# RWKV-7 time mixing on TensorE: key and value products on the off-diagonal quarters, state-free products beside the inverse

## What is computed

```python
def step(s, inp):
    r_t, w_t, k_t, v_t, kk_t, a_t = inp
    sa = jnp.einsum('bhvk,bhk->bhv', s, -kk_t)
    s = (s * w_t[:, :, None, :] + sa[..., None] * (kk_t * a_t)[:, :, None, :]
         + v_t[..., None] * k_t[:, :, None, :])
    return s, jnp.einsum('bhvk,bhk->bhv', s, r_t)
```

## Time and profile before

| | us |
|---|---|
| median of three runs | 5607.72 (5603.7 to 5607.86) |
| the profiled execution | 5603.66 |
| its span, first to last instruction | 5601.9 |

### The profile page before, as it was taken

The page is one execution under the profiler, slowest core; times in us unless marked ns, Lnnn a source line. Parts: engine busy times, 40 slices in busy tenths (PEclk is TensorE's granted clock), DMA queues, the critical chain, the costliest instruction groups (busy, mean ns, idle before and its releaser), DMA issues. The chain is left out here.

```text
span 5601.9 us, 109510 instructions
## 1 busy us (share of the span) xinstructions
PE 5508.0 (98%) x47116; PEld 5411.2 (97%) x47116; DVE 3766.9 (67%) x5137; ACT 2192.3 (39%) x2817; POOL 1360.0 (24%) x902
## 2 busy tenths in 40 slices
PE   8999999999999999989999999999999999999999
PEld 7898999999999999989999999999999999999998
DVE  5676653232357633258887777777778988989898
ACT  4343332222223322122233333334345565555555
POOL 1000000000002200016688888888500000000000
PEclk9999999999999999999999999999999999999999
DMA  3111122232337743323345555555554344353432
GB/s 116 41 54 54 40 94 94 91 115 84 112 107 263 260 155 138 107 82 68 93 100 138 125 116 125 121 123 119 168 191 165 133 150 155 135 177 122 165 133 81
DMA packets 291684, 687.83 MB, mean 123 GB/s; under 512 B 109280, under 2 KB 125024, under 8 KB 268832
## 3 DMA queue, kind: packets, MB, share of 16 engines
q1 hardware_dynamic: 187952, 616.90, 32.5%
q0 software_dynamic: 96128, 45.17, 6.2%
q10 hardware_dynamic: 7152, 19.15, 0.9%
HBM read 564.94 MB, written 116.02 MB: 122 GB/s over the span
## 5 line engine op out<-in xcount | busy, mean ns | idle before, releaser
L2418 POOL DMA_INDIRECT gate_rows<-ah_shares,ah_cells x576 | 1071.4, 1860 | 186.8 <-issue 178.6
L2902 PE MATMUL ps<-va_h_high,va_v_high 128*128 128x288 f32 x3584 | 1056.6, 295 | 6.4 <-DVE va_h_low L140 4.9
L2904 PE MATMUL ps<-va_h_high,va_v_low 128*128 128x288 f32 x3584 | 1058.0, 295 | 0.0
L2903 PE MATMUL ps<-va_h_low,va_v_high 128*128 128x288 f32 x3584 | 1056.9, 295 | 0.0
L2902 PEld LDWEIGHTS ps<-va_h_high,va_v_high 128*128 128x128 f32 x3584 | 673.4, 188 | 7.0 <-DVE va_v_low L140 5.1
L2904 PEld LDWEIGHTS ps<-va_h_high,va_v_low 128*128 128x128 f32 x3584 | 673.5, 188 | 0.0
L2903 PEld LDWEIGHTS ps<-va_h_low,va_v_high 128*128 128x128 f32 x3584 | 673.4, 188 | 0.0
L140 DVE TENSOR_TENSOR ah_ul<-ah_u,ah_uh 128x1024 fp32r<-128x1024 f32 (+1 forms) x344 | 449.6, 1307 | 316.1 <-ACT ah_uh L2359 291.8
L2359 ACT CAST ah_uh<-ah_u 128x1024 fp32r<-128x1024 f32 x324 | 339.8, 1049 | 510.3 <-PE ps L2285 501.0
L2284 PE MATMUL ps<-hn_low,ah_uh 128*128 128x288 f32 x1728 | 511.5, 296 | 0.0
L2285 PE MATMUL ps<-hn_high,ah_ul 128*128 128x288 f32 x1728 | 510.8, 296 | 0.0
(11 more groups left out here) (538 smaller groups left out, 13957.2 us busy)
## 6 DMA issues: line engine op xcount, KB each, us to landing
ah_u<-peer_u SPq DMA_DIRECT2D x216, 512.0 KB, 4.9
va_v<-peer_v SPq DMA_DIRECT2D x96, 1024.0 KB, 7.7
ret_w<-w_ret SPq DMA_DIRECT2D x46, 1024.0 KB, 4.9
gate_rows<-mo_zeros POOLq DMA_DIRECT2D x128, 288.0 KB, 3.9
h_kept<-ah_h SPq DMA_DIRECT2D x128, 288.0 KB
va_g<-gate_rows SPq DMA_DIRECT2D x60, 576.0 KB, 5.7
ah_hidden<-h_kept SPq DMA_DIRECT2D x60, 576.0 KB, 4.9
ah_v<-peer_v SPq DMA_DIRECT2D x30, 1024.0 KB, 5.0
```

What stands on the lines that cost most here:

```text
L2418: pool.indirect_dma_start(cell, bass.IndirectOffsetOnAxis(ap=source[0:m, n, k:k + 1], axis=0), shares[0:m, n, k:k + 1], None, compute_op=A ...
L2902: pe.matmul(z, ah[:, r, f], th[:, q, r, :], start=begin, stop=False, skip_group_check=True)
L2903: pe.matmul(z, ah[:, r, f], tl[:, q, r, :], start=False, stop=False, skip_group_check=True)
L2904: done = pe.matmul(z, al[r][:, f], th[:, q, r, :], start=False, stop=r == R - 1, skip_group_check=True)
```

## The change

Four things, all in `rwkv_stage`.

1. A second helper, `cross`, puts head 0's rows on columns 64 to 127 and head 1's on 0 to 63, the two other quarters. The products of keys and values go there: `kf·pq` in the x phase, the transposes of `kf` and `vs`, `xm·v`, `k·v`. Their results stand with the heads swapped, and the later ones, whose operands are swapped, swap them back.
2. The transposes leave the x phase. The plan of the inverse grows from 14 to 20 products: `tb`, `tk`, `tv` (transposes), `rv`, `yv` (`xm·v` for R and for Y) and `kv` (`k·v`). A product of the five crossed ones stands in one *turn* with the one ahead of it, and a turn's two products alternate chunk by chunk, each in its own bank. ACT evacuates `tb`, `tk`, `tv`; DVE evacuates `rv`, `kv`, `yv` (`kv` times the decay at the chunk's end).
3. The chain loses `k·v` and both `xm·v`. DVE adds their stored results instead: in R and S the `TENSOR_SCALAR` becomes a `SCALAR_TENSOR_TENSOR`, and Y is a DVE addition where ACT copied. R of chunk 0 needs no product. Of the samples, `s8` and one of the two products of `sV` go, and DVE has one more addition in chunk 3.
4. The three pieces after U7 move to x2, x4 and x6, one each. DVE's identity minus `edge` (L967 before) waits for the last `tk`, since it overwrites `kf`.

```diff
     return [
+        ("tb", "pb", "I", "b", None, None),
+        ("tk", "pk", "I", "k", None, None),
         ("f2", "F", "f", "A", "G", None),
+        ("tv", "pv", "I", "v", None, None),
         ("F2", "f", "F", "B", None, None),
         ("f4", "B", "A", "E", None, None),
+        ("rv", "x2", "v", "rv", None, None),
         ("F4", "A", "B", "H", "J", None),
         ("D1", "G", "IF", "L", None, None),
+        ("kv", "k", "v", "kv", None, None),
...
         ("h", "L", "G", "B", None, None),
+        ("yv", "x3", "v", "yv", None, None),
         ("Z", "J", "B", "Z", None, None),
...
-        by_vector = ("F2", "D2", "DT")
-        products = [(n, g) for n in range(len(plan)) for g in range(len(groups))]
+        by_vector = ("F2", "D2", "DT", "rv", "kv", "yv")
+        turns = [[n, n + 1] if n + 1 < len(plan) and plan[n + 1][0] in crossed else [n]
+                 for n in range(len(plan)) if plan[n][0] not in crossed]
+        products = [(n, g) for turn in turns for g in range(len(groups)) for n in turn]
...
-        after = {"a": 4, "g": 2, "ss": 8, "bon": 8, "x": 2, "U1": 4, "U3": 4, "U5": 3, "U7": 3, "Y7": 8, "yT": 2}
+        after = {"a": 4, "g": 2, "ss": 8, "bon": 8, "x2": 1, "x4": 1, "x6": 1, "x": 2, "U1": 4, "U3": 4, "U5": 3, "Y7": 8, "yT": 2}
...
-                for c in range(NCH - 1):
-                    act.wait_ge(pe_s.sem, pe_s.of(i, f"Y{c}"))
-                    act.copy(yy[:, c, :], X[2][:, 0:HEAD]).then_inc(a_s.step(f"Y{c}"), 1)
...
+            def cross(out, lhs, rhs, start=True, stop=True):
+                for r, q in zip(ROWS2, ROWS2[::-1]):
+                    last = pe.matmul(out[q], lhs[r], rhs[r], start=start, stop=stop)
+                return last
...
                     both(x[:, 0:C], pq[:, c, 0, :], part(bb, c))
-                    both(x[:, C:3 * C], part(bb, c), right)
-                    both(x[:, 3 * C:5 * C], part(kf, c), right)
...
-                    both(y[:, 0:C], part(bb, c), eye[:, :])
-                    both(y[:, C:2 * C], part(kf, c), eye[:, :])
-                    both(y[:, 2 * C:3 * C], part(vs, c), eye[:, :]).then_inc(pe_s.step(f"x{c}"), 1)
+                    cross(y[:, C:3 * C], part(kf, c), right)
+                    both(x[:, C:3 * C], part(bb, c), right).then_inc(pe_s.step(f"x{c}"), 1)
+                    if f"x{c}" in after:
+                        fill(i, f"x{c}")
...
-                    both(X[3][:, 0:HEAD], b, uu, start=False).then_inc(pe_s.step(f"S{c}"), 1)
-                    both(X[2][:, 0:HEAD], xm[:, c, 1, :], uu, start=False).then_inc(pe_s.step(f"Y{c}"), 1)
-                    if c < NCH - 2:
-                        both(X[0][:, 0:HEAD], xm[:, c + 1, 2, :], tok[:, c + 1, 2, :], stop=False)
+                    both(X[3][:, 0:HEAD], b, uu, start=(c == 0)).then_inc(pe_s.step(f"S{c}"), 1)
+                    both(X[2][:, 0:HEAD], xm[:, c, 1, :], uu, start=(c == 0)).then_inc(pe_s.step(f"Y{c}"), 1)
...
-                    dve.tensor_scalar(st[:, (c + 1) % 2, :], X[3][:, 0:HEAD], winc[:, end:end + 1], None, ALU.mult)\
-                        .then_inc(v_s.step(f"S{c}"), 1)
-                    dve.drain()
-                dve.wait_ge(a_s.sem, a_s.of(i, f"Y{NCH - 2}"))
+                    dve.scalar_tensor_tensor(out=st[:, (c + 1) % 2, :], in0=X[3][:, 0:HEAD], scalar=winc[:, end:end + 1],
+                                             in1=kv[:, c, :], op0=ALU.mult, op1=ALU.add).then_inc(v_s.step(f"S{c}"), 1)
+                    dve.wait_ge(pe_s.sem, pe_s.of(i, f"Y{c}"))
+                    dve.tensor_tensor(yy[:, c, :], X[2][:, 0:HEAD], yv[:, c, :], ALU.add).then_inc(v_s.step(f"Y{c}"), 1)
+                    dve.drain()
```

More of the change, by code:

```diff
@@ L302, in rwkv_stage @@
         mats = {x: by_chunk(y) for x, y in zip("ABEGHJL", (rs, ks, kk, at, sg, cs, cse))}
+        mats |= {x: tok[:, :, n, :] for n, x in enumerate("bkv")}
+        mats |= {"rv": by_chunk(dif), "kv": by_chunk(vs), "yv": by_chunk(rs)}
+        crossed = ("tk", "tv", "rv", "kv", "yv")
         def part(x, c):
@@ L762, in _ @@
+                    both(x[:, C:3 * C], part(bb, c), right).then_inc(pe_s.step(f"x{c}"), 1)
+                    if f"x{c}" in after:
+                        fill(i, f"x{c}")
                 fill(i, "x")
-                for j, (n, g) in enumerate(products):
-                    name, l, r, _, _, _ = plan[n]
+                for turn, g in [(turn, g) for turn in turns for g in range(len(groups))]:
                     by_act, by_dve = [], []
-                    if j >= 4:
-                        before = label(*products[j - 4])
-                        if before in to_act:
-                            by_act += [before]
-                        else:
-                            by_dve += [before]
-                    elif j >= 2:
-                        by_act += [f"tv{NCH - 1}"]
-                    for m in (l, r):
-                        by = [k for k in range(n) if m in plan[k][3:6]]
-                        if by:
-                            lab = label(by[-1], g)
-                            if m == plan[by[-1]][3] and plan[by[-1]][0] not in by_vector:
-                                by_act += [lab]
-                            else:
-                                by_dve += [lab]
-                    if n == 0:
-                        by_dve += ["il"]
@@ new lines, in _ @@
+                    for n in turn:
+                        name, l, r, _, _, _ = plan[n]
+                        j = turn_no[n, g]
+                        if j >= 4:
+                            before = label(*products[j - 4])
+                            if before in to_act:
+                                by_act += [before]
+                            else:
+                                by_dve += [before]
+                        else:
+                            by_dve += [f"mx{NCH - 1}"]
+                        for m in (l, r):
+                            by = [k for k in range(n) if m in plan[k][3:6]]
+                            if by:
+                                lab = label(by[-1], g)
+                                if m == plan[by[-1]][3] and plan[by[-1]][0] not in by_vector:
+                                    by_act += [lab]
+                                else:
+                                    by_dve += [lab]
+                            elif m == "IF":
+                                by_dve += ["il"]
```

94 lines of the change are left out of this document (51 added, 43 removed).

## The result

| | before | changed |
|---|---|---|
| median of five runs each, us | 5603.7 (5595.36 to 5607.86) | 5637.99 (5629.72 to 5642.51) |
| the profiled execution, its span | 5603.66, 5601.9 | 5639.64, 5637.8 |
| ratio, changed to before | | 1.006 (95%: 1.0045 to 1.0075) |

The kernel became slower by 34 us, 0.6%. That lies in the range given (5602 to 5650) and on the side that was given 60%, but it is nearly four times the 9 us of the case held likeliest, and outside that case's own range (5608 to 5626).

The account below looks back on a forecast made before the run. PE, busy 98% of the span, was taken as the bound. Per pair, x phase -1.5, inverse +5.4 and chain -2.8 us gave +1.1, +9 in all: 5617 us against the median, with 8 in 10 from 5602 to 5650.

Parts of the forecast that it names:

- B: Rival: only wide products overlap, so the inverse pays for crossed products; +2.9 us a pair, 5631 us; chance 20%.
- C: Rival: crossed products wait for their partners in x phase and inverse; +4.7 us a pair, 5645 us; chance 21%.
- case A: Likeliest case: four quarters run at once, crossed products cost nothing; +1.1 us a pair, 5617 us (5608 to 5626); 45%.
- Four quarters at once: PE array: a crossed product beside its partner costs nothing (likelier) or its full time, 0.22 us wide, 0.12 narrow.
- x phase: Before the inverse: cheaper chunks, three single pieces added; 8.7 us against 10.2, minus 1.5 a pair.
- Chain: Last of the three stages costed: round trips over DVE shorten little, minus 2.8 us a pair in all.
- U7 to S7: End of the chain: without the pieces after U7 this step falls from 2.83 us to 0.66, minus 2.17.
- R0: Start of the chain: rn comes from stored rv, so U0 stands 0.05 us behind the sample product, minus 0.82.
- Case D: Rival, faster: removed products shorten the chain (2.4 us a pair) or half the bank waits go (2.2); 5598 or 5580; 12%.
- The waits for banks: Inverse: PE waits for evacuations because turns fill two of four banks per group; 4.05 us walked, 4.4 taken.
- The inverse: Twenty products in fifteen turns: one more turn 1.05 us, crossed products 0, bank waits 4.4; plus 5.4 a pair.
- The clock: Closing remark: a granted clock below 1.00 in these stages would make the forecast wrong; no size or chance given.

## Why the prediction was right in sign and short in size

The measured 5638 us lies inside the stated range by luck. The range went up to 5650 to make room for B and C, in which crossed products cost time, and they don't; case A, whose mechanism held, ended at 5626. The same goes for the side: 41 of the 60% for slower came from B and C, and A alone leaned to no difference. What made the kernel slower by so much were two terms that the sum didn't have.

- **Four quarters at once: right.** Price of a crossed product beside its partner: nothing. Partners start 0.01 us apart on the same rows, the wide ones of the x phase (231.79 and 231.80) and the narrow ones of the inverse (243.86 and 243.87, [f4,rv]), and a group of both narrow products takes 0.36 us. B and C fall, although the median came out between their two times (5631 and 5645): their longer groups are found only in the run with all products on the diagonal.
- **x phase: right,** -1.3 for -1.5.
- **Chain: right,** -2.9 for -2.8, with its parts: U7 to S7, R0, and nothing for the products between R and U. Case D falls with that.
- **The waits for banks: right.** Second pair: 1.3 + 1.09 + 0.75 + 1.5 is 4.6 us, against 4.05 walked and 4.4 taken; and the run with another order on DVE took two of them away.
- **The inverse: a term was missing.** Plus 6.9 where 5.4 was said. Nearly all of the difference is the supply of instructions, 1.4 us a pair, 11 us in all. The step that failed is in the inverse's working: five crossed products "cost 0" because the array has room for them. The change put 1717 matmuls and loads into the two stages where there had been 1465, in a kernel whose two stages already ran at 58 of them per us. The earlier trace rows had the numbers: 505 matmuls and 506 loads in 15.19 us are 67 per us, in the densest stage, and the change makes groups twice as dense. (The inverse of before kept up those 67 per us without a hole over 0.4 us, so the 59 per us on which I built later expectations is a mean over both stages of the kernels with holes, not a limit of every stretch.)
- **The clock: the step that failed most.** "U7 to S7 ... falls to the 0.66, minus 2.17" is true, and the sentence behind it, that the eight pieces stay, took their length for granted. The stretch behind the last Y was in no window of the prediction. It grew by 12.6 us in all, 11.7 of them by the clock and 0.9 by the late cast. The last sentence of the prediction named a granted clock below 1.00 as a thing that would make it wrong, but gave it no price and no chance. What the runs show in place of that sentence: moving the pieces in the kernel before leaves the clock up, and so does putting thrown-away products into the chain of the changed one; taking the products out with the pieces left behind U7 lowers it in two or three of eight pairs, and both edits together in six.

Together: 9 forecast, 11 from the supply, 12.6 behind the last Y, and some 3 in later stages, of 36 between the two profiled executions.

What stays open: why the clock held with 9 or 10 small products a chunk and fell at the end of four to eight of the eight chains with 6 and 8 and no pieces behind U7, beyond that it did; and the 3 us of the later stages, which the change doesn't touch. In those the traces differ in how long the granted clock is at 0.5 (78 us before, 85 in the changed kernel, 52 to 86 in the other runs), so they are no effect of the change that I could show. An estimate from these: 6.5 us more at half the clock cost up to 3.3 us, which is all of the rest.

## What to carry to other kernels

Before products are moved out of a chain of round trips because they are "free of the state", ask what they cost there: two of the three here cost 0.1 us a pair, and in the dense stage to which they went they cost banks, DVE evacuations and instructions. Where PE issues many small matmuls, count its instructions per us as a resource beside the array; when a stretch is near the rate of supply (here 256 instructions in 3.9 to 4.8 us), a second product on free quarters only brings the end of the block sooner. And whenever work leaves a stretch that is half idle, look at the clock of the stretch behind it, which may lose more than was saved: by the table, moving the pieces from U7 to the x phase saved some 0.4 us a pair in the two stages and the chain, and the stretch behind them took 1.6 more.

## What the runs showed of the hardware

- Two fp32 products of 64x64 on all four quarters of the array, written to separate banks, run at the same time: first starts 0.01 to 0.02 us apart, a group of three chunks in 0.36 us for both products (0.70 on the diagonal).
- PE's instructions come in blocks of 256, one packet of 16 KB; all 13 holes over 0.4 us in the changed kernel's x phases and inverses stood at the same count modulo 256, and ended 1.2 to 1.6 us behind the end of a packet. A block that ended in such a hole took 3.9 to 4.8 us from the start of one to the next, and no pair of any run got above 61 matmuls and loads per us over its two stages (most: 1679 in 27.7 us). A single stage did: 67 per us over the 15.19 us of the inverse of before, with no such hole.
- PE's clock was 1.00 through chains in which it had nine or ten products of 64 columns a chunk of 2.0 us and fell to 0.5, for 3.4 or 6.8 us at a time, at the end of four to eight of the eight chains of each kernel with six or eight and no pieces behind U7. With six and the pieces there it fell in two and three of the eight, ahead of the pieces. In three kernels the nine or ten included products with no reader, and the clock stayed at 1.00.
